# Seven-product tile pairs in the last gated up stage of a four-block network, and conditioning products in other slots

## What is computed

```python
def conv_ffn(h, w_up, conv_w, conv_b, w_down):
    up = h @ w_up
    up = lax.conv_general_dilated(
        up, conv_w[:, None, :], window_strides=(1,), padding=[(CONV_W - 1, 0)],
        dimension_numbers=('NWC', 'WIO', 'NWC'), feature_group_count=2 * D_FF_2) + conv_b
    val, gate = jnp.split(up, 2, axis=-1)
    return (jax.nn.silu(gate) * val) @ w_down
...
    cond = jax.nn.silu(c)
    for i in range(DEPTH):
        mod = cond @ ada_w[i] + ada_b[i]
```

## Time and profile before

| | us |
|---|---|
| median of 3 runs (1679.23 to 1680.6) | 1679.47 |
| the profiled execution: time | 1679.56 |
| the profiled execution: span of the trace | 1677.8 |
| PE busy in the span | 1633.3 (97%) |
| DVE busy | 1003.7 (60%) |
| ACT busy | 353.7 (21%) |
| the chain that ended last, share of PE | 88% |
| `up0` from pair 2 to its end | 244.8 to 373.9 |
| `up3` from pair 2 to its end | 1463.6 to 1601.8 |

### The profile page before, as it was taken

How to read it: one execution, slowest core, us unless ns; L and a number is a source line. 1 busy time by engine, 2 the same in 40 slices (tenths; PEclk the granted TensorE clock), 3 DMA queues, 4 the chain that set the end, 5 groups by cost and what they waited for, 6 DMA issues and landing times.

```text
span 1677.8 us, 27211 instructions
## 1 busy us (share of the span) xinstructions
PE 1633.3 (97%) x10888; PEld 1428.4 (85%) x10888; DVE 1003.7 (60%) x2086; ACT 353.7 (21%) x825; POOL 73.2 (4%) x86
## 2 busy tenths in 40 slices
PE   7999999999989999999999999999999999999998
PEld 6758889999978867788899786688889998888898
DVE  6554668888655334586767577556645683434455
ACT  3241212220151102100001322422213131222200
POOL 0000000000000000195000000000000000000000
PEclk9999999999999999999999999999999999999999
DMA  6445467776545584667654343245444503455545
GB/s 226 141 145 193 179 217 251 245 223 227 189 161 157 193 319 138 237 238 275 213 169 170 90 118 109 76 149 153 150 139 164 176 3 113 140 152 153 154 169 189
DMA packets 79901, 289.50 MB, mean 173 GB/s; under 512 B 8992, under 2 KB 10016, under 8 KB 79264
## 3 DMA queue, kind: packets, MB, share of 16 engines
q1 hardware_dynamic: 79776, 287.76, 52.2%
HBM read 286.68 MB, written 1.05 MB: 171 GB/s over the span
## 4 chain that ended last, share of the span: by engine, by line
PE 88%; DVE 8%; DMA 2%; issue 1%; ACT 1%; SPq 0%; DVEq 0%; ACTq 0%
PE acc L480 46%; PE acc L611 16%; PE acc L669 4%; PE acc L571 4%; PE acc L1134 3%; PE acc L535 2%; PE acc L556 1%; DVE big L2178 1%; DMA ring<-stream 1%; PE acc L490 1%; PE acc L1113 1%; PE score L1099 1%; PE acc L751 1%; DVE bT L2002 1%; PE score L775 1%
## 5 line engine op out<-in xcount | busy, mean ns | idle before, releaser
L480 PE MATMUL acc<-H,ring 128*128 128x256 f32 x2864 | 631.1, 381 | 12.3 <-DMA ring<-stream 8.3
L480 PEld LDWEIGHTS acc<-H,ring 128*128 128x128 f32 x2864 | 544.1, 191 | 95.0 <-DMA ring<-stream 9.7
L480 PE MATMUL acc<-big,ring 128*128 128x256 f32 x880 | 192.2, 379 | 0.9 <-PE acc L480 0.9
L480 PEld LDWEIGHTS acc<-big,ring 128*128 128x128 f32 x880 | 166.8, 190 | 24.8 <-issue 2.3
L2291 DVE SCALAR_TENSOR_TENSOR pair<-acc,cols,pair 128x255 f32<-128x255 f32 x84 | 40.5, 483 | 114.9 <-ACT pair L1380 110.7
L2002 DVE SCALAR_TENSOR_TENSOR bT<-bT,cond 128x1024 f32<-128x1024 f32 x64 | 83.3, 1302 | 39.5 <-DMA bT<-ada_in 34.1
L1784 DVE TENSOR_TENSOR probs_t<-ring 128x512 f32<-128x512 f32 (+1 forms) x96 | 62.1, 647 | 58.5 <-PE acc L611 52.7
L611 PE MATMUL acc<-FFN,ring 128*128 128x128 f32 x760 | 93.6, 275 | 0.0
L611 PEld LDWEIGHTS acc<-FFN,ring 128*128 128x128 f32 x760 | 89.1, 192 | 0.6 <-issue 0.4
L1380 ACT ACTIVATE pair<-acc,cols 128x256 f32<-128x256 f32 x84 | 47.1, 564 | 164.5 <-PE acc L480 164.5
L1212 ACT ACTIVATE SQ<-X 128x256 f32<-128x256 f32 x56 | 23.4, 417 | 181.3 <-DVE X L1760 107.4
(11 more groups left out here) (510 smaller groups left out, 2205.7 us busy)
## 6 DMA issues: line engine op xcount, KB each, us to landing
ring<-stream SPq DMA_DIRECT2D x440, 512.0 KB, 3.6
bT<-ada_in SPq DMA_DIRECT2D x76, 512.0 KB, 5.0
big<-ada_in SPq DMA_DIRECT2D x20, 512.0 KB, 4.8
big<-ssm_in SPq DMA_DIRECT2D x2, 1024.0 KB, 6.5
cols<-cols_in SPq DMA_DIRECT2D x1, 1165.5 KB, 9.8
X<-x_in SPq DMA_DIRECT2D x4, 256.0 KB, 5.4
MEM<-mem_in SPq DMA_DIRECT2D x1, 1024.0 KB, 12.7
y_out<-X SPq DMA_DIRECT2D x8, 128.0 KB, 3.6
```

Of the source, the lines that this page charges most:

```text
L480: mm = nc.tensor.matmul(dst, w[:, k * cols_per:(k + 1) * cols_per], r, start=first and n == 0, stop=last and n == len(src) - 1)
```

## The change

- `up3`: pairs 2 to 21 with k % 3 != 1, fourteen in all, run through `quick_pair`. The pairs 1, 4, 7, ..., 19 stay plain. On DVE the turn of pair k is now: sums for pair k + 1 if it is a product pair, gating of pair k - 2, taps of pair k - 1, joining of pair k if it is a product pair. On ACT: three part copies of pair k, one copy of the last half of pair k - 1, the fourth part copy of k, Silu of k - 2, first taps of k - 1.
- The sums of the first weight chunk of `down0` and `down3` go to another buffer (`Q`) and come before the last gated tile of the up stage.
- The conditioning blocks: the same 96, behind other slots. In `up0` the turns 9 and 17 have none, turn 0 one and turn 1 two; `od_xb` has two fewer and `xq1` two more; in `up1` the turns with two are 8 to 13 in place of 0, 3, 5, 8, 9, 10.

```diff
-ADA_TWICE = (0, 3, 5, 8, 9, 10)
+ADA_TWICE = (8, 9, 10, 11, 12, 13)
+ADA_UP0 = (0, 1, 1) + tuple(k for k in range(2, 21) if k not in (9, 17))
 ADA_SLOTS = [
     ("ev_out", range(0, 8, 2)), ("xq0", (1, 2, 3, 4, 5, 6, 7, 7)), ("xo0", range(0, 8, 2)),
-    ("up0", range(2, 42, 2)), ("down0", (0, 2, 4, 8, 10, 14)),
-    ("od_xb", (0, 1, 6, 7)),
-    ("xq1", (0, 1)), ("xk1", range(8)), ("xv1", range(8)), ("xo1", range(0, 8, 2)),
+    ("up0", [2 * k + e for e, k in zip((0, 0, 1) + (0,) * 17, ADA_UP0)]), ("down0", (0, 2, 4, 8, 10, 14)),
+    ("od_xb", (0, 1)),
+    ("xq1", (0, 1, 2, 3)), ("xk1", range(8)), ("xv1", range(8)), ("xo1", range(0, 8, 2)),
     ("up1", [2 * k + e for k in range(22) for e in range(2 if k in ADA_TWICE else 1)]),
...
-QUICK = [("up0", 2, 22)]
-QUICK0, QUICK_SLOT = {}, {}
-_pairs = 0
-for _name, _lo, _hi in QUICK:
-    QUICK0[_name] = _pairs - _lo
-    for _j in range(_lo, _hi):
-        QUICK_SLOT[SLOT0[_name] + 2 * _j] = QUICK_SLOT[SLOT0[_name] + 2 * _j + 1] = QUICK0[_name] + _j
-    _pairs += _hi - _lo
...
+QUICK = {"up0": range(2, 22), "up3": [k for k in range(2, 22) if k % 3 != 1]}
+QUICK_AT, QUICK_SLOT = {}, {}
+for _name, _js in QUICK.items():
+    for _j in _js:
+        QUICK_SLOT[SLOT0[_name] + 2 * _j] = QUICK_SLOT[SLOT0[_name] + 2 * _j + 1] = QUICK_AT[_name, _j] = len(QUICK_AT)
...
+QUICK_BEFORE = {f"down{n[-1]}": max(q for (m, _), q in QUICK_AT.items() if m == n) + 1 for n in QUICK}
...
-        summed_weights = [probs_t[:, 0:512], probs_t[:, 512:1024], pair[:, 0:512], pair[:, 512:1024]]
+        def summed_weights(name):
+            homes = ((Q, 0), (Q, 512), (Q, 1024), (Q, 1536)) if name in QUICK_BEFORE else \
+                ((probs_t, 0), (probs_t, 512), (pair, 0), (pair, 512))
+            return [x[:, lo:lo + 512] for x, lo in homes]
...
-                for k in range(2, 2 * quick_from(name)):
+                for k in range(2, 44):
+                    if (name, k // 2) in QUICK_AT:
+                        if k % 2 == 0:
+                            quick_pair(name, k // 2, H)
+                        continue
...
+            def quick_conv_ffn(name, layer):
+                i = layer + 2
+                begin(name)
+                def first_tap(k):
+                    act.wait_ge(ffn_mid, k + (22 * i + 1))
+                    if (name, k) in QUICK_AT:
+                        act.wait_ge(pair_out, QUICK_AT[name, k] + 1)
+                    for e in range(2):
+                        c = k + (22 if e == 0 else 0)
+                        if k == 0:
+                            lead_waits(1)
+                            src = at(FFN, 10 + e)
+                        elif (name, k) in QUICK_AT:
+                            src = at(quick_out(QUICK_AT[name, k]), e)
+                        else:
+                            act.wait_ge(slot_used, RING + SLOT0[name] + 1 + k * 2 + e)
+                            src = acc[(TILE0[name] + 2 * k + e) % 4][:, 0:S]
+                        nc.scalar.activation(at(pair, 2 * (k % 2) + e), src, ACT.Identity, bias=col("fconv_b", c + 44 * layer),
+                                             scale=col("fconv_w", c + (3 * layer + 2) * 44)).then_inc(conv_first, 1)
+                def gate(k):
+                    act.wait_ge(taps_out, k + 1)
+                    nc.scalar.activation(at(pair, 2 * (k % 2)), at(pair, 2 * (k % 2)), ACT.Silu).then_inc(silu_done, 1)
+                for k in range(24):
+                    quick = (name, k) in QUICK_AT
+                    if quick:
+                        keep_parts(name, k)
+                    if (name, k - 1) in QUICK_AT:
+                        q = QUICK_AT[name, k - 1]
+                        act.wait_ge(pair_steps, 5 * q + 5)
+                        act.wait_ge(taps_out, k - 1)
+                        own(nc.scalar.activation(quick_out(q)[:, HALF:S], acc[(TILE0[name] + 2 * k - 2) % 4][:, P:2 * P],
+                                                 ACT.Copy))
+                        act.sem_inc(acc_free, 1)
+                    if quick:
+                        keep_part(QUICK_AT[name, k], 3, acc[(TILE0[name] + 2 * k) % 4])
+                    if k >= 2:
+                        gate(k - 2)
+                    if 1 <= k < 23:
+                        first_tap(k - 1)
...
+                    elif name in QUICK_BEFORE:
+                        dve.wait_ge(pair_steps, 5 * QUICK_BEFORE[name])
...
-                    ada(2)
+                    ada(4)
...
+            def combine_pair(name, j, tiles_apart):
+                q, t = QUICK_AT[name, j], TILE0[name] + 2 * j
                 parts, out_of = kept(q), quick_out(q)
+                first, last = (halves(out_of[:, 0:2 * S])[:, 0:4:2, :], out_of[:, 3 * P:4 * P]) if tiles_apart else \
+                    (halves(out_of[:, 0:2 * P]), out_of[:, 2 * P:3 * P])
...
+                for k in range(2, 22):
                     if k < 21:
                         sum_pair(name, k + 1)
-                    if k > first:
+                    if k > 2:
                         gated_tile(k - 1)
-                    if k < 21:
-                        ada(1)
-                    combine_pair(name, k)
+                    ada(ADA_UP0.count(k))
+                    combine_pair(name, k, False)
+                sum_weights(f"down{layer}", 0)
                 gated_tile(21)
...
+            def quick_conv_ffn(layer):
+                name, i = f"up{layer + 2}", layer + 2
+                inverse_rms(rstd[:])
+                lead_norm(gained_in_ffn, rstd[:], lambda k: mod_col(layer, 3, k))
+                begin(name)
+                def taps(k):
+                    for e in range(2):
+                        c = k + (22 if e == 0 else 0)
+                        quick = (name, k) in QUICK_AT
+                        b = at(FFN, 10 + e) if k == 0 else at(quick_out(QUICK_AT[name, k]), e) if quick else \
+                            acc[(TILE0[name] + 2 * k + e) % 4]
+                        z = (2 * (k % 2) + e) * S
+                        dve.wait_ge(conv_first, k * 2 + (8 + 44 * layer + e + 1))
+                        own(v.scalar_tensor_tensor(pair[:, z + 1:z + S], b[:, 0:S - 1], col("fconv_w", c + (3 * layer + 1) * 44),
+                                                   pair[:, z + 1:z + S], ALU.mult, ALU.add))
+                        own(v.scalar_tensor_tensor(pair[:, z + 2:z + S], b[:, 0:S - 2], col("fconv_w", c + 3 * layer * 44),
+                                                   pair[:, z + 2:z + S], ALU.mult, ALU.add))
+                        if not quick:
+                            dve.sem_inc(acc_free, 1)
+                    dve.sem_inc(taps_out, 1)
+                def gated_tile(k):
+                    dve.wait_ge(silu_done, k + (44 + 8 + 22 + 1))
+                    own(v.tensor_tensor(at(FFN, k), at(pair, 2 * (k % 2)), at(pair, 2 * (k % 2) + 1), ALU.mult))
+                    dve.sem_inc(ffn_mid, 1)
+                    if k in (8, 16):
+                        sum_mids(i, k // 8 - 1)
+                for k in range(22):
+                    if k == 0:
+                        for e in range(2):
+                            shifted_lead_tile(name, e, at(FFN, 10 + e), rstd[:])
+                            dve.sem_inc(lead_out, 1)
+                        sum_tokens(H)
+                    if (name, k + 1) in QUICK_AT:
+                        sum_pair(name, k + 1)
+                    if k >= 2:
+                        gated_tile(k - 2)
+                    if k >= 1:
+                        taps(k - 1)
+                    if (name, k) in QUICK_AT:
+                        combine_pair(name, k, True)
+                sum_weights(f"down{i}", 0)
+                gated_tile(20)
+                taps(21)
+                gated_tile(21)
+                sum_mids(i, 2)
+                paired_residual(f"down{i}", lambda k: mod_col(layer, 5, k))
...
-                if k >= 4:
+                if k in (5, 6):
...
-            conv_ffn(1)
+            quick_conv_ffn(1)
...
```

## The result

| | before | after |
|---|---|---|
| median of 4 runs each, us | 1679.35 (1678.24 to 1680.6) | 1714.16 (1712.08 to 1718.19) |
| ratio, 95% interval | | 1.021 (1.0187 to 1.0232) |
| profiled execution: time / span, us | 1679.56 / 1677.8 | 1712.08 / 1709.9 |
| PE busy in the span, us | 1633.3 | 1639.8 |

What follows compares the result with a forecast made beforehand. PE, busy 97% of the span, was taken as the bound, so any new wait costs fully. up3 +28.9, down3 +2.4 and conditioning -8.0 gave +23.3 on 1679.56: 1702.9 us, range 1691.5 to 1711.

Steps and rivals of the forecast that it cites:

- Direction, place, number of waits: In up3, PE idles 5.8 us before pair 2 and about 3.2 us before pairs 3, 6, ..., 21; slower overall.
- the mid sums: In up3, sums behind gated tiles 8 and 16 make DVE late in two turns, 0.65 us each, 1.3 us.
- A product pair saves 0.65: In up3, a pair as seven products takes 6.26 us of PE instead of 6.91, if PE never waits.
- The clock: In up3, idles bring slow restarts of 1.6 us: one at pair 2, plus four of the seven others, 6.4 us.
- Rival 1: All seven 3.2 to 3.3 us idles in up3 bring the lower clock: +11.2 instead of +6.4, 1707.7 us; chance 0.20.
- Into `down3`: Behind up3, the first sum of down3's second chunk comes after 12.6 us instead of 10.1: loss 2.4 us.
- The conditioning blocks: New places: od_xb -5.9, xq1 +5.2, up1 -5.3, up0 -2.0, together -8.0 us.
- B: In up3, the second product pair after a plain one (3, 6, ..., 21), forecast to wait about 3.2 us for banks.
- By its order: In up3, DVE limits through the order of its work, not its load, some 16 us of 22.7 per three pairs.
- ACT is not later: In up3, ACT's first taps of a plain pair end 6.5 us into the next pair; DVE wants them at 7.2.
- rival 3: In up3, plain pairs' taps beat PE if load and sums (6.4 us) leave the chain: 1662.5 us; chance 0.05.

Runs made afterwards that it cites:

- e4: Changed kernel plus unread PE matmuls before the eight bank waits of up3 (50 before pair 2, 26 before the others), longer than the idles: 1717.12 us.
- e5: Changed kernel plus unread PE matmuls sized to fit the eight idles of up3 (24 before pair 2, 13 before the others): 1696.77 us.
- e1: Changed kernel with up3 back to plain products and its old order, new conditioning places kept: 1669.56 us, 0.9939 of the kernel before.
- e12: Changed kernel with DVE's taps of a plain pair moved ahead of the weight sums, ACT's order left as it was: 1686.81 us.
- e11: Changed kernel with plain pairs' DVE taps and ACT first tap ahead, two xq1 loads moved to slots 4 and 5, thirteen up3 product pairs: 1662.87 us.
- e2: Changed kernel with the conditioning products back in their old places, up3 product pairs kept: 1724.90 us, 1.0267 of the kernel before.

## Why the prediction was right and wrong

- **Direction, place, number of waits: right.** Eight waits where they were put, ended by DVE's second tap; 29.5 us were forecast (5.8, seven times 3.2, 1.3 for the mid sums, which took 1.0 each and not 0.65). The idle is 30.8; with the uncovered ends of the groups, which the forecast's way of counting has in the waits, it is 32.1, 2.6 more.
- **A product pair saves 0.65: right.** e4 closes to 0.1 us with it.
- **The clock: the step that failed.** It was put at the first fall and four of seven, 1.6 us each, 8.0 in `up3`. All eight came, and the eight restarts took 15.8, 2.0 each. Of the 7.8 us missing, 4.8 are the number of falls and 3.0 their price, which I had read from the one tile at 472.49. The price is not one number: 1.5 to 1.7 us in five cases, 2.4 and 2.5 behind the two idles of 4.25 us, but 2.7 behind pair 3's of 3.28 and only 1.6 behind the longest, 5.96. e5 shows the term as a whole, 16.2 us in `up3`. Rival 1 had the number of falls and not the price, so the range ended too low.
- **Into `down3`: half of it.** 2.77 us of wait at the second chunk, 2.4 forecast. That this idle would bring a slow restart like the others was left out: 4.7 in all.
- **The conditioning blocks: right.** -5.5, +5.1 and -5.0 against -5.9, +5.2 and -5.3; `up0` brought 3.7 in place of 2.0, both of its idles of the earlier trace rows went whole. Together -9.1 for -8.0; e1 alone has -10.2.
- **Luck.** The idle of 2.76 us at the norm stands in all fourteen traces. A slow stretch followed it in eight of them, before's among these, and none in six, after's among these: 2.2 us that no edit explains.
- **What bounds B.** "By its order" was right for DVE, and so was "ACT is not later" for this kernel (6.15 us against 7.41). But rival 3's condition (load and sums off the chain) was not enough: e12 has it and still waits 1.67 us, now for ACT. ACT's order had to change as well.

The profiled executions miss 8.8 us: 7.8 from the clock in `up3`, 2.6 from its longer waits, 2.3 from `down3` and 0.4 elsewhere, less 1.1 from the conditioning blocks, 2.2 of luck, 0.5 at the first load and 0.5 of rounding in the forecast's own sum: 8.8.

## What to carry to other kernels

Before an engine's queue gets work that waits for a load, put what frees somebody's buffer ahead of it, on every engine of the chain; then look what the moved work itself waits for, and which engine is the next limit. Price an idle of PE at its length plus the restart, and set the two apart by filling it. One stage's extra sums (here the mid sums) are a turn of their own: work out the turns behind them, not only the regular one.

## What the runs showed of the hardware that I had not expected

A restart of PE at the lower clock is not a fixed price and not a fixed rule. In `up3` over all kernels: waits of 0.64 to 1.68 us were never followed by slow instructions; of 1.81 to 2.06 us sometimes (the two rows of e11 above have the same 1.89 us, 4.54 and 2.92 us for the same 24 instructions); of 2.95 us and more always but once. The exception is e2's pair 3, idle 3.29 us, with a granted clock of 1.00 over the 3 us that follow, where the same pair in after, idle 3.28 us, had 0.50. Outside `up3` the idle in `xq1` is another: 3.52 us in e1 and the clock stays at 1.00, 3.31 us in after and it is 0.50. The rows are e2's and e1's:

```profile
1482.14 2.02 PE L666 MATMUL acc<-H,ring 128*128 128x128 f32 x16 [3.29 <-DVEq L2382]
...
553.67 17.58 PE L477 MATMUL acc<-H,ring 128*128 128x256 f32 x80 [3.52 <-DMA ring<-stream]
```

Of the 26 idles of 2.95 us and more in `up3`, over all kernels, that one stayed warm and 25 did not, so four falls of seven was too few. Behind the idle of 2.76 us of the earlier trace rows it was eight of fourteen.

The Trainium skill (TensorE: Matmul & The Clock Gate, Part 1) has the array's clock halved after idle time, which rival 1 went by; these traces agree with it behind most waits of 2.95 us and more, with the two exceptions above, and the 16 to 17 us of e5 are its size here.
